# Attention with four banks for scores, one bank for dense results, and denominators inverted in eight columns before they are spread

## The reference, cut to what matters

```python
s = einsum('bqgrd,bqkgd->bqgrk', qg, kg) * scale      # scores
s = where(valid, s, -inf)
p = softmax(s, axis=-1)
o = einsum('bqgrk,bqkgd->bqgrd', p, vg)
...
a = dsa_attention(q, k, v, qi, ki, wi, k_sel) * silu(z_a)
y = g[:, :, 0] * (a @ w_branch_a) + g[:, :, 1] * (b @ w_branch_b)
x = x + y @ w_out
```

## Time and profile before

| | |
|---|---|
| median of 3 runs (lowest, highest) | 3717.32 us (3714.79, 3723.7) |
| the profiled execution's own time | 3715.48 us |
| its span in the profile | 3713.6 us |
| TensorE (PE) busy in the span | 3559.7 us, 96% |
| VectorE busy | 1959.5 us, 53% |
| ScalarE busy | 1585.8 us, 43% |

### The profile page before, as it was taken

The page is one execution under the profiler, slowest core; times in us unless marked ns, Lnnn a source line. Parts: engine busy times, 40 slices in busy tenths (PEclk is TensorE's granted clock), DMA queues, the critical chain, the costliest instruction groups (busy, mean ns, idle before and its releaser), DMA issues. The chain is left out here.

```text
span 3713.6 us, 68764 instructions
## 1 busy us (share of the span) xinstructions
PE 3559.7 (96%) x27852; PEld 2692.3 (72%) x27852; DVE 1959.5 (53%) x4802; ACT 1585.8 (43%) x3591; POOL 420.7 (11%) x689
## 2 busy tenths in 40 slices
PE   6999999978999999989999999999999999999998
PEld 5887777856666666568777887777886676676765
DVE  4223333337777777434678788666673343443332
ACT  2222332224444444213677666777753334443320
POOL 0000000004444444210000000000000000000000
PEclk9999999988999999999999999999999999999999
DMA  9111111133222222231111114121215212111121
GB/s 301 53 52 50 49 52 52 52 116 128 74 74 74 74 74 74 88 128 47 48 53 51 61 51 163 55 65 54 69 62 173 74 49 76 41 48 65 44 78 47
DMA packets 137250, 282.10 MB, mean 76 GB/s; under 512 B 26368, under 2 KB 85648, under 8 KB 130448
## 3 DMA queue, kind: packets, MB, share of 16 engines
q1 hardware_dynamic: 130208, 268.88, 20.5%
q0 software_dynamic: 2304, 8.39, 0.6%
q10 hardware_dynamic: 4464, 1.02, 0.1%
HBM read 181.78 MB, written 96.47 MB: 75 GB/s over the span
## 5 line engine op out<-in xcount | busy, mean ns | idle before, releaser
L2506 ACT ACTIVATE at_pT<-at_bank 128x512 f32<-128x512 f32 (+3 forms) x320 | 154.4, 531 | 574.2 <-PE at_bank L2401 573.8
L272 PEld LDWEIGHTS p_bank<-p_hT,w_in 128*128 128x128 f32 x3328 | 378.6, 193 | 12.1 <-issue 9.9
L272 PE MATMUL p_bank<-p_hT,w_in 128*128 128x128 f32 x3328 | 383.2, 276 | 2.1 <-ACT p_hT L365 2.1
L1907 PEld LDWEIGHTS p_bank<-p_hT,w_in_rest 128*128 128x128 f32 x3072 | 345.4, 192 | 14.0 <-issue 12.4
L1907 PE MATMUL p_bank<-p_hT,w_in_rest 128*128 128x128 f32 x3072 | 349.9, 276 | 1.3 <-DVE p_st L2184 1.3
L2029 ACT ACTIVATE p_r<-p_acc,p_mid 128x384 f32<-128x384 f32 (+13 forms) x224 | 292.8, 1307 | 59.4 <-DVE p_acc L2211 55.0
L278 PE MATMUL p_bank<-w_in,p_hT 128*128 128x512 f32 (+2 forms) x1024 | 312.3, 463 | 0.0
L2524 DVE CUSTOM_DVE_ANT_0 at_s<-at_bank,at_bias 128x512 f32<-128x512 f32 (+3 forms) x320 | 181.8, 606 | 189.5 <-PE at_bank L2388 182.9
L278 PEld LDWEIGHTS p_bank<-w_in,p_hT 128*128 128x128 f32 x1024 | 172.0, 191 | 117.2 <-issue 107.1
L1057 PE MATMUL b_banks<-b_wout,b_yT 128*128 128x512 f32 x512 | 248.0, 610 | 3.7 <-DVE b_yT L1390 2.2
L2442 PE MATMUL at_bank<-arena,at_y 128*128 128x512 f32 x512 | 245.4, 602 | 2.9 <-DVE at_y L2552 2.5
(11 more groups left out here) (400 smaller groups left out, 5848.3 us busy)
## 6 DMA issues: line engine op xcount, KB each, us to landing
stage<-p_st SPq DMA_DIRECT2D x16, 1856.0 KB, 5.9
arena<-stage SPq DMA_DIRECT2D x16, 1856.0 KB, 7.7
at_rest<-stage SPq DMA_DIRECT2D x16, 1280.0 KB, 6.0
stage<-p_pr SPq DMA_DIRECT2D x128, 128.0 KB, 1.8
p_ada<-in_ada_w SPq DMA_DIRECT2D x4, 2048.0 KB, 15.8
p_xt<-in_x SPq DMA_DIRECT2D x16, 512.0 KB, 3.4
b_x<-in_x SPq DMA_DIRECT2D x16, 512.0 KB, 3.4
x<-b_x SPq DMA_DIRECT2D x16, 512.0 KB, 2.9
```

What stands on the lines that cost most here:

```text
L272: last = mm(out, w_in[:, k, place(c):place(c) + P], hT[:, k, 1:P + 1], start=(k == 0), stop=(k == KD - 1))
L1907: last = mm(bank[:, m * P:(m + 1) * P], weights(k, c + m * P, c + (m + 1) * P), hTs[:, n % 2, k, :], start=(k == 0), stop=(k == KD - 1))
```

## The change

It does these things, all in `attention`:

- `FRONT` gets four banks instead of two, two for each of two blocks in flight; a block's scores wait for the masks of the block two earlier instead of the one just before.
- PE issues the scores' blocks in runs of two: blocks 0 and 1, then (TD and) values, then blocks 2 and 3. TD comes ahead of the values.
- After the scores four dense pieces follow in one run; the other four are dealt out between the transposes.
- `SPARE` gets one bank instead of three: every dense use now waits until the use before it has been taken out.
- VectorE inverts the eight denominators of a row (8 columns) and then copies them to 512 columns, instead of inverting 512 columns. `mask` is cut in two parts, blocks 0 and 1 and blocks 2 and 3, and `join_heads` stands between them at c = 0.

```diff
-        FRONT, TURNED, OUT, SPARE = B[0:2], B[2:4], B[4], B[5:8]
+        FRONT, TURNED, OUT, SPARE = B[0:4], B[4:6], B[6], B[7]
...
                 def spare_for(n, use):
                     k = 7 * n + SPARE_USE.index(use)
-                    if k >= 3:
-                        pe.wait_ge(S["spare_taken"], k - 2)
-                    return SPARE[k % 3]
+                    from_one(pe, S["spare_taken"], k)
+                    return SPARE
...
-                            from_one(pe, S["masked"], 2 * (j - 1) + g + 1)
+                            from_one(pe, S["masked"], 2 * (j - 2) + g + 1)
...
                     pieces = scores(step + 1) if step + 1 < STEPS else iter(())
                     others = dense(n - 1, c) if finishing else iter(())
                     next(pieces, None)
+                    next(pieces, None)
+                    if finishing and c == 0:
+                        turn_denominators(n - 1)
                     if 0 <= step - 1 < STEPS:
                         values(step - 1)
-                    if finishing and c == 0:
-                        turn_denominators(n - 1)
-                    next(pieces, None)
-                    left = 8
-                    for _piece in range(len(blocks(ORDER[(step + 1) // PAIRS_A])) - 2 if step + 1 < STEPS else 0):
+                    for _piece in pieces:
+                        pass
+                    for _piece in range(4):
                         next(others, None)
-                        next(others, None)
-                        next(pieces, None)
-                        left -= 2
                     if 0 <= step < STEPS:
-                        for _piece in range(left - len(blocks(ORDER[n]))):
-                            next(others, None)
                         for _turned in turn_probabilities(step):
-                            next(others, None)
+                            for _piece in range(-(-4 // len(blocks(ORDER[n])))):
+                                next(others, None)
                     for _piece in others:
                         pass
...
                     if n >= 1 and c == 0:
                         dve.wait_ge(S["probs"], 2 * step)
-                        v.reciprocal(rden[:, :, :], spread(den[:, (n - 1) % 2, :].unsqueeze(2), [P, 8, HEAD])).then_inc(S["rden_ready"], 1)
+                        v.reciprocal(rnum[:, :], den[:, (n - 1) % 2, :]).then_inc(S["rden_small"], 1)
+                        dve.wait_ge(S["rden_small"], n)
+                        v.tensor_copy(rden[:, :, :], spread(rnum[:, :].unsqueeze(2), [P, 8, HEAD])).then_inc(S["rden_ready"], 1)
                     if step + 1 < STEPS:
-                        mask(step + 1)
+                        mask(step + 1, 0)
+                    if n >= 1 and c == 0:
+                        join_heads(n - 1)
+                    if step + 1 < STEPS:
+                        mask(step + 1, 1)
```

More of the change, by code:

```diff
@@ L2311, in attention @@
         mx, nm = sb("mx", [P, 2, 4]), sb("nm", [P, 2, 8])
-        den, rden = sb("den", [P, 2, 8]), sb("rden", [P, 8, HEAD])
+        den, rnum, rden = sb("den", [P, 2, 8]), sb("rnum", [P, 8]), sb("rden", [P, 8, HEAD])
         zR, aT = sb("zR", [P, 4, P]), sb("aT", [P, 4, P])
@@ L2385, in scores @@
                         for g in range(2):
-                            from_one(pe, S["masked"], 2 * (j - 1) + g + 1)
+                            from_one(pe, S["masked"], 2 * (j - 2) + g + 1)
                             rows = slice(64 * g, 64 * g + 64)
-                            last = mm(FRONT[g][:, 0:w], qT[rows, n % 2, c, :], KT[rows, at:at + w], start=True, stop=True)
+                            last = mm(FRONT[2 * (j % 2) + g][:, 0:w], qT[rows, n % 2, c, :], KT[rows, at:at + w], start=True, stop=True)
                         last.then_inc(S["scores"], 1)
@@ L2511, in _, with mask @@
                 tt = v.tensor_tensor
-                def mask(step):
+                def mask(step, part):
                     n, c = step // PAIRS_A, step % PAIRS_A
                     nb = len(blocks(ORDER[n]))
[L2516 to L2521, removed]
+                    if part == 0:
+                        if c == 0:
+                            dve.wait_ge(S[f"bias_loaded{n % 2}"], 16 * (n // 2 + 1))
+                        from_one(dve, S["turned"], 2 * blocks_before(step - 1) if step >= 1 else 0)
+                        from_one(dve, S["probs"], 2 * (step - 1))
+                    for kb, (at, w) in list(enumerate(blocks(ORDER[n])))[2 * part:2 * part + 2]:
+                        j = blocks_before(step) + kb
+                        dve.wait_ge(S["scores"], j + 1)
@@ L2522, in mask @@
                         for g in range(2):
                             least = mx[:, g, kb:kb + 1] if nb > 1 else nm[:, n % 2, 2 * c + g:2 * c + g + 1]
-                            v.tensor_tensor_reduce(out=s[:, step % 2, g, at:at + w], in0=FRONT[g][:, 0:w], in1=bias[:, n % 2, at:at + w], scale=HEAD ** -0.5, scalar=3.0e38,
+                            v.tensor_tensor_reduce(out=s[:, step % 2, g, at:at + w], in0=FRONT[2 * (j % 2) + g][:, 0:w], in1=bias[:, n % 2, at:at + w], scale=HEAD ** -0.5, scalar=3.0e38,
@@ L2525, in mask @@
                                                    op0=ALU.add, op1=ALU.min, accum_out=least).then_inc(S["masked"], 1)
[L2526 to L2531, removed]
+                    if part == 1:
+                        dve.wait_ge(S["masked"], 2 * blocks_before(step + 1))
+                        if nb > 1:
+                            v.tensor_reduce(nm[:, n % 2, 2 * c:2 * c + 2], mx[:, :, 0:nb], AX.X, ALU.min).then_inc(S["row_max"], 1)
+                            dve.wait_ge(S["row_max"], step + 1)
+                        else:
+                            dve.sem_inc(S["row_max"], 1)
@@ L2535, in join_heads @@
                     dve.wait_ge(S["za_loaded"], 64 * (n + 1))
-                    tt(flat(zR[:, :, :]), SPARE[7 * n % 3][:, :], za[:, :], ALU.mult).then_inc(S["spare_taken"], 1)
+                    tt(flat(zR[:, :, :]), SPARE[:, :], za[:, :], ALU.mult).then_inc(S["spare_taken"], 1)
                     dve.wait_ge(S["spare_taken"], 7 * n + 1)
@@ L2545, in gate_b @@
                     dve.wait_ge(S["rest_loaded"], 16 * (n + 1))
-                    tt(flat(yb[:, 4 * half:4 * half + 4, :]), SPARE[k % 3][:, :], gates[:, 1024 + half * 512:1536 + half * 512], ALU.mult).then_inc(S["spare_taken"], 1)
+                    tt(flat(yb[:, 4 * half:4 * half + 4, :]), SPARE[:, :], gates[:, 1024 + half * 512:1536 + half * 512], ALU.mult).then_inc(S["spare_taken"], 1)
                 def gate_a(n, half):
@@ L2551, in gate_a @@
                     dve.wait_ge(S["spare_done"], k + 1)
-                    tt(mine, SPARE[k % 3][:, :], gates[:, half * 512:half * 512 + 512], ALU.mult).then_inc(S["spare_taken"], 1)
+                    tt(mine, SPARE[:, :], gates[:, half * 512:half * 512 + 512], ALU.mult).then_inc(S["spare_taken"], 1)
                     dve.wait_ge(S["spare_taken"], k + 1)
@@ L2561, in finish @@
                     dve.wait_ge(S[f"x_loaded{n % 2}"], 16 * (n // 2 + 1))
-                    tt(o[:, n % 2, c], SPARE[k % 3][:, :], o[:, n % 2, c], ALU.add).then_inc(S["spare_taken"], 1)
+                    tt(o[:, n % 2, c], SPARE[:, :], o[:, n % 2, c], ALU.add).then_inc(S["spare_taken"], 1)
                 for step in range(-1, STEPS + PAIRS_A):
@@ L2567, in _ @@
                         dve.wait_ge(S["probs"], 2 * step)
-                        v.reciprocal(rden[:, :, :], spread(den[:, (n - 1) % 2, :].unsqueeze(2), [P, 8, HEAD])).then_inc(S["rden_ready"], 1)
+                        v.reciprocal(rnum[:, :], den[:, (n - 1) % 2, :]).then_inc(S["rden_small"], 1)
+                        dve.wait_ge(S["rden_small"], n)
+                        v.tensor_copy(rden[:, :, :], spread(rnum[:, :].unsqueeze(2), [P, 8, HEAD])).then_inc(S["rden_ready"], 1)
                     if step + 1 < STEPS:
-                        mask(step + 1)
+                        mask(step + 1, 0)
[3 more added lines that the diff above has]
+                        mask(step + 1, 1)
                     if n >= 1:
                         if c == 0:
-                            join_heads(n - 1)
                             gate_b(n - 1, 0)
```

## The result

| | before | after |
|---|---|---|
| median (4 runs each) | 3717.89 us | 3681.73 us |
| lowest, highest | 3714.79, 3723.7 | 3680.89, 3684.25 |
| span of the profiled execution | 3713.6 us | 3679.1 us |
| waits of PE for `rden` | 19.8 us, 12 times | 3.7 us, 4 times |
| stretches at half clock inside the stage, each behind a wait for `rden` | 4 | 1 |

The changed kernel is faster: ratio 0.9904, interval 0.989 to 0.9918, some 36 us. I had forecast 3694, in a range of 3680 to 3707.

What follows compares the result with a forecast made beforehand. PE bounds the attention stage, busy 895 of 925.5 us. Gains of 46.3 less costs of 23.6 give -22.7 against the profiled 3715.5, so 3692.8; with the median 1.8 above that execution, forecast 3694, range 3680 to 3707.

Steps and rivals of the forecast that it cites:

- Boundaries, 21.4: PE's switches between array layouts: 64 fewer runs of scores at 0.20 us and 45 fewer full-array runs at 0.19, gain 21.4.
- Rival A: Score blocks in a run save nothing among themselves: boundary gain only 8.6, time 3707; half of it 3700; chance 0.09.
- TD, 13.9: PE's waits for the inverted denominators ahead of TD fall from 20.2 us to 6.3, with TD starting 1.84 into its step.
- Masks, 7.8: Score blocks no longer wait for the previous block's masks: 5.5 us at c = 0, 2.3 after short values.
- Clock, 3.2: Two of four half-clock stretches behind long waits for `rden` go, at 1.6 us each: gain 3.2 us.
- The single bank, 19.0: PE waits between dense halves until VectorE empties the one bank: 16.0 us in halves, 2.4 drain, 0.6 tile 0.
- join_heads, 4.6: `b0` waits for `join_heads`, now behind two blocks' masks: 4.6 us over tiles 4, 6, 8, 7, 5, 0 and drain.
- Rival C: VectorE, still in masks when a half ends, delays the single bank, 1.2 us at 32 changes: 3732, slower; chance 0.04.
- Rival B: Half the single bank's cost goes (9.5 us) and two more clock stretches return (3.2): 3681; chance 0.16.

## Why the prediction was right, and where it was off

The prediction's sum was -46.3 + 23.6 = -22.7 against the profiled execution; the spans differ by 34.5. All the starts below are those of the profile after, unless another is named.

1. *Boundaries, 21.4.* Right. The block inside a run pays no front and no end (1.92 for two, 1.91 forecast), and parting 16 places cost 6.2 to 6.9 against 6.3. Rival A, with its 3707 or 3700, is out. So is the strict reading of the Trainium skill, TensorE: Matmul & The Clock Gate (Part 3, The mechanism): by it each inner block would keep 0.1, and two blocks would take 2.02, where the trace has 1.92.
2. *TD, 13.9.* Somewhat low. The sum for TD's start was 1.84 and measured 1.52: the copy holds VectorE 0.43 and not 0.69, and `finish` starts 0.11 into the step in the small tiles and not 0.17. PE follows the copy by 0.15, as it followed the inversion. TD's waits came to 4.1 by the starts (0.5, 0.9, 1.1 and 1.6 at tiles 3, 1, 0 and the drain) and not 6.3. The thirteen waits before come to 20.8 when each run of values is held against its length without a wait, and not to 20.2, so the gain is 16.7. I had taken a two-operand row for the copy, and the other bound that I gave was nearer. The trace of the kernel before had a nearer row too, 512 columns of one tensor, multiplied by a number, on the same store, at 485 ns:

```profile
L2196 DVE TENSOR_SCALAR p_acc<-p_r,p_wi 128x512 f32<-128x512 f32 x28 | 13.2, 485 | 60.5 <-ACT p_r L2081 59.7
```

The Trainium skill, VectorE: DVE Perf Modes (The perf-mode tier table), had the copy at twice the rate. The trace agrees once the fixed part is allowed for: masks of 128 and of 512 columns take 286 and 685 ns on average, which is 0.15 fixed and 0.53 for 512 columns, and 0.15 with half of 0.53 is 0.42, against 0.43.
3. *Masks, 7.8.* Right: no line of PE's waits names a mask any more.
4. *Clock, 3.2.* Low: three of four stretches went, 4.8. The one left lies in the drain, behind TD's wait of 1.6 and the one of 0.41 for its bank.
5. *The single bank, 19.0.* This is the term that was off most. The sum for one exposure was 1.21, with 0.15 from VectorE's end to PE. It measured 0.27 + 0.69 + 0.06 (3183.42) + 0.10 = 1.12, so where eight transposes cover it the cost is 0.13 + 0.10 = 0.23 and not 0.34. By the starts the halves in the tiles cost 10.2 and not 13.6, the drain 4.6 and not 4.8, tile 0 0.4: 15.2 in all. The 0.15 was read where PE waits for `rden`, and I used it for a wait for a bank. These two differ, whatever the instruction's length; in the drain:

```profile
3634.93 0.63 PE L2450 MATMUL at_bank<-ident,at_rden 128*128 128x128 f32 x4 [1.45 <-DVE at_rden L2570]
...
3642.64 3.84 PE L2430 MATMUL at_bank<-at_rest,at_wb 128*128 128x128 f32 x32 [0.84 <-DVE at_yb L2546]
...
3634.35 0.43 DVE L2570 COPY at_rden<-at_rnum 128x512 f32<-128x512 f32 x1
...
3641.90 0.69 DVE L2546 TENSOR_TENSOR at_yb<-at_bank,at_rest 128x512 f32<-128x512 f32 x1 [4.89 <-PE at_bank L2430]
```

PE goes on 0.15 behind the end of the copy of 0.43 us, and 0.05 behind the end of the instruction of 0.69 that emptied the bank. The first of the twelve waits for `rden` before, at tile 4, had 0.06 as well, so the difference holds for most of these waits and not for all; why I leave open.
6. *join_heads, 4.6.* It measured 2.5 by the starts: 1.0, 0.7, 0.3 and 0.5 at tiles 4, 6, 0 and the drain, and nothing at tiles 8, 7 and 5. The masks began earlier by the 0.3 of point 2.

With the measured sizes: 21.3 + 16.7 + 7.8 + 4.8 - 15.2 - 2.5 = 32.9 of the stage's 33.8. Another 0.8 lies at the stage's first blocks, which no longer wait for masks, and the rest is within the rounding. The 11.8 us by which the forecast sum fell short are therefore no single step of it: the single bank is 3.8 of them, TD 2.8, `join_heads` 2.1, the clock 1.6, the first blocks 0.8, and 0.7 lies ahead of the stage.

What the prediction didn't stress is how much hangs on the inversion. Terms 2 and 4 do, and the 5.5 of term 3, 22.6 as forecast; the other 2.3 of term 3 need the four banks, for with the short inversion alone those waits stay (a block of 256 keys behind short values takes 1.10 there too, at 3509.66). The 33 of the inversion alone are by its starts 19.2 of TD's waits, 5.2 of the blocks behind TD, 6.3 of clock, and the 1.7 at the stage's beginning that aren't the edit's: 32.4 together. In the old order the values cover more of TD's wait than in the new one (1.6 left, not 4.1), and the fourth half-clock stretch goes as well. The runs' 21.4 were real too, and the single bank that pays for them, with what the move of TD adds, took nearly all of it. That the two cancel was in my numbers, but I had not set them side by side, and named no rival in which the inversion is nearly the whole change.

Rival C, the single bank as the bound, was refuted where it was to show. VectorE's waits in the stage (32 `gate_b` and 32 of `gate_a`'s first instruction):

```profile
DVE at_yb L2546 <- PE at_bank L2430: 121.3, 32, 6.5
DVE at_y L2552 <- PE at_bank L2430: 114.4, 32, 5.9
```

It waited for PE ahead of every one of the 64, so it was never in masks when a half ended. Rival B came nearest, 3681, but its reasons hold only in part: PE follows the bank's release sooner and one more stretch of clock comes back, which is 3.8 and 1.6 us where it had 9.5 and 3.2. That its number was met so closely is chance.

## What to carry to other kernels

An instruction on an engine that is 53% busy can cost more than all the reordering around it brings, if it stands alone between the last result of one tile and the first need of the next: look what a single wait by the bounding engine is made of, before its order is rewritten. When a change trades buffers for runs, price the two apart, and ask at which moments the buffers given up stand idle elsewhere; lending them at those moments brought 15 us, and lending one at the wrong moment gave back 11.5 of it. Work that lies between two uses of a double buffer is cover for whoever empties it, and can't be moved for another's sake without a look at that engine.

## What the runs showed of the hardware that I had not expected

The copy of 8 columns to 512 with a repeated source took 0.43 us, though all 512-column instructions of VectorE around it take 0.69. The inversion of 8 columns took 0.19 and that of 512 took 3.34, so by these two it costs some 6.3 ns for each column, against 0.69 us for a whole multiplication of 512. In all four waits for `rden` after the change PE went on 0.15 us behind the end of the copy, and 0.05 to 0.06 behind an instruction that only emptied its bank (3183.42 and 3642.64). Stretches at half clock, with a loss of 1.6 us each, came with the long waits for `rden`: there were four before, none with the short inversion alone, and ten with the long inversion in the new order, two of them twice as long as the others, which is part of why that kernel is slower than before. With three banks in the small tiles there was none either, though TD's wait of 1.44 us in the drain was still there.
